# Nine norm totals of a two-layer encoder kernel: from an fp32 product with ones to two fp32r products of a split sum, one slab later

## The reference, cut to what matters

```python
def layer_norm(x, g, b):
    mu = jnp.mean(xf, axis=-1, keepdims=True)
    var = jnp.mean(jnp.square(xf - mu), axis=-1, keepdims=True)
    y = (xf - mu) * lax.rsqrt(var + LN_EPS)
...
    h = causal_dwconv(h, conv_w, conv_b)
    h = jax.nn.silu(layer_norm(h, conv_ln_g, conv_ln_b))
...
        x = layer_norm(DN_ALPHA * x + (1.0 + gate) * y, ln1_g[l], ln1_b[l])
```

## Time and profile before

| | |
|---|---|
| median of 3 runs | 2107.39 us (2107.19 to 2108.32) |
| the profiled execution: its own time | 2107.35 us |
| its span, first to last instruction | 2105.4 us |
| PE busy | 2070.4 us (98%) |
| POOL busy | 1406.3 us (67%) |
| DVE busy | 1189.1 us (56%) |
| ACT busy | 1025.9 us (49%) |
| mean granted TensorE clock | 0.996 |

### The profile page before, as it was taken

The page is one execution under the profiler, slowest core; times in us unless marked ns, Lnnn a source line. Parts: engine busy times, 40 slices in busy tenths (PEclk is TensorE's granted clock), DMA queues, the critical chain, the costliest instruction groups (busy, mean ns, idle before and its releaser), DMA issues.

```text
span 2105.4 us, 27351 instructions
## 1 busy us (share of the span) xinstructions
PE 2070.4 (98%) x9619; PEld 1701.4 (81%) x9619; DVE 1189.1 (56%) x1945; ACT 1025.9 (49%) x1834; POOL 1406.3 (67%) x1773
## 2 busy tenths in 40 slices
PE   7999999999999999999999999999999999999997
PEld 6877778787888888888788888888778888888887
DVE  5888888575515554777632545687651454333235
ACT  3585356555516674374633656234552464433332
POOL 4987767856677887875567885564546776545554
PEclk9999999999999999999999999999999999999999
DMA  8654545533434354553233333332323232434332
GB/s 300 157 134 147 160 128 147 163 110 101 120 110 124 107 162 145 140 159 94 75 105 100 118 103 93 99 106 71 101 73 108 87 104 83 128 100 128 93 93 78
DMA packets 421508, 250.06 MB, mean 119 GB/s; under 512 B 48149, under 2 KB 393085, under 8 KB 421373
## 3 DMA queue, kind: packets, MB, share of 16 engines
q1 hardware_dynamic: 420506, 248.03, 40.1%
q10 hardware_dynamic: 867, 0.29, 0.1%
HBM read 242.71 MB, written 4.26 MB: 117 GB/s over the span
## 4 chain that ended last, share of the span: by engine, by line
PE 80%; POOL 8%; DVE 4%; ACT 4%; issue 3%; DMA 1%; SPq 0%; POOLq 0%; ACTq 0%; DVEq 0%
PE fg L862 25%; PE fg L864 25%; PE fg L863 25%; POOL w_lo L1884 4%; POOL ada_acc L1955 1%; PE bank_s L948 1%; DVE bank_c L1496 1%; ACT ada L1283 1%; DMA stage_in<-in_x_dram 1%; PE bank_l L874 1%; PE bank_t L970 1%; PE bank_l L885 1%; PE bank_t L957 0%; ACT w_hi L1127 0%; POOL ssum L1978 0%
## 5 line engine op out<-in xcount | busy, mean ns | idle before, releaser
L1884 POOL TENSOR_TENSOR w_lo<-raw,w_hi 128x256 fp32r<-128x256 f32 (+1 forms) x1425 | 1032.3, 756 | 626.7 <-ACT w_hi L1127 625.2
L862 PE MATMUL fg<-u_hi,w_hi 128*128 128x512 f32 x2112 | 838.6, 397 | 5.8 <-DVE u_lo L1476 2.1
L864 PE MATMUL fg<-u_hi,w_lo 128*128 128x512 f32 x2112 | 823.7, 390 | 0.0
L863 PE MATMUL fg<-u_lo,w_hi 128*128 128x512 f32 x2112 | 823.4, 390 | 0.0
L1127 ACT ACTIVATE w_hi<-raw 128x1024 fp32r<-128x1024 f32 (+2 forms) x387 | 375.6, 970 | 386.5 <-PE fg L864 282.9
L862 PEld LDWEIGHTS fg<-u_hi,w_hi 128*128 128x128 f32 x2112 | 397.0, 188 | 103.9 <-issue 16.2
L864 PEld LDWEIGHTS fg<-u_hi,w_lo 128*128 128x128 f32 x2112 | 397.0, 188 | 84.6
L863 PEld LDWEIGHTS fg<-u_lo,w_hi 128*128 128x128 f32 x2112 | 397.4, 188 | 81.8 <-issue 2.6
L1496 DVE SCALAR_TENSOR_TENSOR bank_c<-glu,par,bank_c 128x512 f32<-128x512 f32 x448 | 306.1, 747 | 0.1
L1838 DVE SCALAR_TENSOR_TENSOR x<-fg,mod,x 128x512 f32<-128x512 f32 (+1 forms) x168 | 121.6, 724 | 320.0 <-PE fg L864 319.8
L864 PE MATMUL fg<-h_hi,w_lo 128*128 128x512 f32 (+1 forms) x704 | 269.8, 383 | 0.0
(11 more groups left out here) (264 smaller groups left out, 1846.2 us busy)
## 6 DMA issues: line engine op xcount, KB each, us to landing
raw<-in_w_up_dram SPq DMA_DIRECT2D x176, 512.0 KB, 3.8
ada<-in_w_ada_ffn_dram SPq DMA_DIRECT2D x48, 512.0 KB, 4.5
raw<-in_w_down_dram SPq DMA_DIRECT2D x64, 384.0 KB, 3.4
raw<-in_w_in_dram SPq DMA_DIRECT2D x40, 512.0 KB, 3.9
raw<-in_w_down_dram SPq DMA_DIRECT2D x64, 320.0 KB, 3.1
ada<-in_w_ada_mix_dram SPq DMA_DIRECT2D x32, 512.0 KB, 4.3
raw<-in_w_in_dram SPq DMA_DIRECT2D x32, 256.0 KB, 3.8
raw<-in_w_out_dram SPq DMA_DIRECT2D x32, 256.0 KB, 2.9
```

Of the source, the lines that this page charges most:

```text
L862: pe.matmul(out, hi[:, k, :], rhi, start=k == order[0], stop=False)
L863: pe.matmul(out, hi[:, k, :], rlo, start=False, stop=False)
L864: ins = pe.matmul(out, lo[:, k, :], rhi, start=False, stop=k == order[-1])
L1884: ins = pool.tensor_tensor(lo_of(n)[:, ks, :], raw[n % NRAW][:, ks, :], hi_of(n)[:, ks, :].bitcast(F32), ALU.subtract)
```

## The change

For the nine norms, the sum is split before it is totalled. A new step `ch` or `xh` takes the slab that `cm` or `xm` had. In it ACT waits for the finished `ssum` and copies it, rounded, to `sum_hi` (fp32r), and POOL then subtracts `sum_hi` from `ssum` into `sum_lo` (fp32r). `cm` or `xm`, and with it all of `cc` or `xc`, moves one slab on; there PE waits for `sum_lo` and makes two fp32r products with a matrix of ones (`ones_r`), high and low, into the same bank. `cv`, `xv` and what follows keep their slabs. c0 and x0 keep the fp32 product. The entries of c1, x2 and c3 leave `INSIDE`. `sum_lo` takes the memory of `ssum` and `sum_hi` that of `wide`; `ones_r` takes that of three small tiles of the tail and some more.

```diff
 INSIDE = {("cm", 0): 2, ("cv", 0): 4, ("xm", 0): 4, ("xr", 0): 6,
-          ("cm", 1): 2, ("xm", 2): 4, ("cm", 3): 2, ("as", 12): 2, ("as", 18): 2}
+          ("as", 12): 2, ("as", 18): 2}
...
     def conv_norm(mi, ns):
         m, v, r, o = ns
-        put(m, "cm", mi)
+        put(m, "ch", mi)
+        put(m + 1, "cm", mi)
         for k in range(CT):
-            put(m, "cc", mi, k)
+            put(m + 1, "cc", mi, k)
...
     def x_norm(xi, m, c, v, r, per):
-        put(m, "xm", xi)
+        put(m, "xh", xi)
+        put(m + 1, "xm", xi)
         for k in range(DT):
-            put(m + k // c, "xc", xi, k)
+            put(m + 1 + k // c, "xc", xi, k)
...
+            def total_of_parts(n):
+                pe.wait_ge(set_par, 4)
+                pe.wait_ge(total_lo, n)
+                pe.matmul(bank_l[:], ones_r[:], sum_hi[:], start=True, stop=False)
+                return pe.matmul(bank_l[:], ones_r[:], sum_lo[:], start=False, stop=True)
...
             def x_stat(what, xi):
                 if what == "xm":
-                    pe.wait_ge(xsum, (DT - 1) * (xi + 1))
                     take("l", xcenter, DT * (xi + 1))
-                    total().then_inc(xstat, 1)
+                    if xi:
+                        total_of_parts(PARTED["x", xi]).then_inc(xstat, 1)
+                    else:
+                        pe.wait_ge(xsum, DT - 1)
+                        total().then_inc(xstat, 1)
...
+            def sum_high(turn):
+                act.wait_ge(*summed(turn))
+                act.wait_ge(*spread_before(turn))
+                act.activation(sum_hi[:], ssum[:], ACT.Copy).then_inc(total_hi, 1)
...
+            act.activation(ones_r[:], ones_1, ACT.Copy).then_inc(set_par, 1)
...
+                    elif what in ("ch", "xh"):
+                        sum_high((what[0], step[1]))
...
+            def sum_low(turn):
+                pool.wait_ge(total_hi, PARTED[turn])
+                pool.tensor_tensor(sum_lo[:], ssum[:], sum_hi[:].bitcast(F32), ALU.subtract).then_inc(total_lo, 1)
...
+                    elif what in ("ch", "xh"):
+                        sum_low((what[0], step[1]))
```

More of the change, by code:

```diff
@@ L158 @@
          ("x", 5), ("x", 6), ("x", 7)]
+NORM_TURNS = [t for t in TURNS if t[0] != "i"][:-1]
+PARTED = {t: n + 1 for n, t in enumerate(t for t in NORM_TURNS if t[1])}
 NCHUNK = 3 * D // T
@@ L479, in build @@
         tmp = sb("tmp", [P, 2, T])
+        with ExitStack() as region:
+            sum_lo = sb("sum_lo", [P, T], F32R, stack=region)
+            sum_hi = sb("sum_hi", [P, T], F32R, stack=region)
         ssum = sb("ssum", [P, T])
@@ L495, in build @@
         st = sb("st", [P, 2, 7, QT])
-        stats = sb("stats", [P, TB, 2, 6])
-        moments = sb("moments", [P, TB, 2])
-        shift = sb("shift", [P, 2, TB])
+        with ExitStack() as region:
+            stats = sb("stats", [P, TB, 2, 6], stack=region)
+            moments = sb("moments", [P, TB, 2], stack=region)
+            shift = sb("shift", [P, 2, TB], stack=region)
+        ones_r = sb("ones_r", [P, P], F32R)
         with ExitStack() as region:
@@ L584, in build @@
         tr_done, t_copied, pv_done, ahi, alo = (sem(n) for n in ("tr_done", "t_copied", "pv_done", "att_hi", "att_lo"))
+        total_hi, total_lo = sem("total_hi"), sem("total_lo")
         in_const, in_taps, in_sinks, in_pos, tab_out = (sem(n) for n in ("in_const", "in_taps", "in_sinks", "in_pos", "tab_out"))
@@ L631, in freeing, with summed, spread_before @@
             return freed[FREE[P_][0]], FREE[P_][1]
+        def summed(turn):
+            kind, i = turn
+            return (csum, (CT - 1) * (i + 1)) if kind == "c" else (xsum, (DT - 1) * (i + 1))
+        def spread_before(turn):
+            kind, i = NORM_TURNS[NORM_TURNS.index(turn) - 1]
+            return (cstat if kind == "c" else xstat), 3 * (i + 1)
         def copied(c):
@@ L913, in c_stat @@
                 if what == "cm":
-                    pe.wait_ge(csum, (CT - 1) * (mi + 1))
                     take("l", ccenter, CT * (mi + 1))
-                    total().then_inc(cstat, 1)
+                    if mi:
+                        total_of_parts(PARTED["c", mi]).then_inc(cstat, 1)
+                    else:
+                        pe.wait_ge(csum, CT - 1)
+                        total().then_inc(cstat, 1)
                 elif what == "cv":
```

## The result

The changed kernel takes 2123.84 us (median of 4 runs, 2123.15 to 2125.48) beside 2107.29 for the kernel before (4 runs, 2106.84 to 2108.32): a ratio of 1.0081, 95% interval 1.0068 to 1.0094. It is slower, as forecast, but by 16.6 us where 6.2 were forecast, and outside the range of 2109 to 2117.5.

The account below looks back on a forecast made before the run. PE was taken to bound the kernel, busy 2070.4 of 2105.4 us. Savings of 9.3 us against 4.1 of products, 9.0 of waits and 2.5 of restarts gave +6.3 us: 2113.6 us forecast, range 2109 to 2117.5.

Parts of the forecast that it names:

- What goes: PE at the nine norms: dropping the fp32 totals, with their waits for the sum, saves 9.3 us.
- The products and waits: PE at the nine totals: two fp32r products each add 4.1 us in all; eight waits for `sum_lo` add 9.0 us.
- Starting again: PE behind each of eight waits for `sum_lo`: 0.31 us lost before full flow, 2.5 us in all.
- The long stop: An earlier, longer PE wait for an activation part, whose 0.31 us loss was taken as the price of each restart.
- The sum on PE: Savings, new products, waits and restarts at the nine totals together: +6.3 us on PE.
- costed at nothing: ACT's copies, POOL's subtractions, squares a slab later, the copy of `ones_r` and the shifted memory layout: no cost.
- No wait: Rival at the totals: POOL's subtraction ends before PE comes, only savings and new products remain; 2102.2 us, 8%.
- Absorbed: Rival: PE's later stops shrink by what it now waits at the totals, no change; 2109 us, 13%.
- Later waits too: Rival: squares a slab later reach `xv` or `cv` late, at two to four norms by 1 to 2 us; 2116 to 2120 us, 10%.

Follow-up runs that it names:

- b_moved: Kernel before with the nine fp32 totals one slab later and none inside a slab, nothing split: 2106.77 us, ratio 0.9998.
- a_pad64: Changed kernel with 64 bytes of padding behind `ones_r`, so `h` lies 256 bytes from its old place: 2113.04 us, ratio 1.003.
- b_pad192: Kernel before with an empty 192-byte tile ahead of the convolution tiles, shifting `h` as the change did: 2118.75 us, ratio 1.0055.
- a_hi_only: Changed kernel with 64 bytes of padding behind `ones_r`, PE making only the high product, POOL's subtraction unused: 2101.6 us, ratio 0.9976.
- a_late2: Changed kernel with 64 bytes of padding behind `ones_r`, totals done behind the 2nd tile of the slab after the next: 2104.08 us, ratio 0.9986.
- a_late4: Changed kernel with 64 bytes of padding behind `ones_r`, totals done behind the 4th tile of the slab after the next: 2104.17 us, ratio 0.9986.
- b_w_off32: Kernel before with 32 bytes of padding ahead of the weight tiles and 32 behind them: 2151.25 us, ratio 1.021.
- b_all_off64: Kernel before with 64 bytes of padding behind `x`, so `u`, the weights and `h` move together: 2107.97 us, ratio 1.0003.
- b_pad64: Kernel before with an empty 64-byte tile ahead of the convolution tiles: 2111.15 us, ratio 1.0023.
- b_w_off192: Kernel before with 192 bytes of padding ahead of the weight tiles and 64 behind them: 2121.89 us, ratio 1.0071.
- b_w_off64: Kernel before with 64 bytes of padding ahead of the weight tiles and 64 more behind them: 2141.87 us, ratio 1.0168.
- b_pad128: Kernel before with an empty 128-byte tile ahead of the convolution tiles: 2118.88 us, ratio 1.0062.
- b_u_off64: Kernel before with `u` moved by 64 bytes, the weights and `h` by 128: 2138.27 us, ratio 1.0151.

## Why the prediction failed in its size

**What goes: right.** The steps between last products show what the nine totals cost before and what stands in the next slab now (us):

| | c1 | x1 | x2 | c2 | x3 | x4 | c3 | x5 | x6 | sum |
|---|---|---|---|---|---|---|---|---|---|---|
| removed, measured | 0.90 | 1.09 | 1.23 | 0.87 | 1.09 | 0.90 | 1.25 | 1.09 | 0.90 | 9.3 |
| removed, forecast | 0.87 | 1.10 | 1.21 | 0.87 | 1.10 | 0.90 | 1.21 | 1.10 | 0.90 | 9.3 |
| added, measured | 1.25 | 1.98 | 2.01 | 0.45 | 2.05 | 1.89 | 0.96 | 1.99 | 1.84 | 14.4 |
| added, forecast | 1.28 | 2.16 | 2.24 | 0.45 | 2.16 | 2.00 | 1.06 | 2.16 | 2.00 | 15.5 |

**The products and waits: right.** Two products cost 0.45 (c2, which does not wait, shows them alone). The eight waits come to 8.5 us for 9.0; x1 waits 1.29 for 1.40, since the chain from the end of slab 102 to the end of the subtraction is 641.29 - 634.33 = 6.96 us, not 7.07. POOL's subtraction takes 1.26 to 1.29 us; the 1.1 estimated from the Trainium skill's "GPSIMD Engine Reference", section 3.1, does not hold for it.

**Starting again: too large.** Forecast 0.31 a wait, 2.5 in all. Left of 14.4 after waits (8.5) and products (4.1) is 1.8 us, 0.22 each. At x1 the second product starts at 641.75, 0.46 behind POOL's end, where 0.23 would be full flow. The long stop was not the right price. The Trainium skill's rule that PE's queue can pull a weight load ahead ("TensorE: Matmul & The Clock Gate", the array as 16 sub-arrays) is not what made it smaller: the load began at 641.41, only when the wait was over.

**The sum on PE: nearly right.** At the totals +5.1 where +6.3 was forecast. To that come two knock-ons of 0.7 and 0.25 us. Neither was in the sum. The 0.7 is PE's wait for POOL's modulation sum at slab 130; b_moved has it too (0.8 us by the starts), without any subtraction, so it belongs to the later place of the norms. The prediction named these sums, but looked at loads and squares, not at the PE step that reads them. The 0.25 at slab 182 is not in b_moved, but in all kernels that split the sum; no run here tests its cause. The changed kernel without its shift, a_pad64, takes 2113.04 us; the forecast was 2113.6. That they are so near is in part luck: in the trace of a_pad64 the nine places give 5.4 us, 0.9 under the forecast, and the two knock-ons give the 1.0 back.

**The step that failed** is the last of what was costed at nothing: "The memory layout moves by less than a tile; no row prices that, nothing from below and nothing from above is what I take, as no instruction changes its shape". Shape was the wrong thing to look at. A shift of 192 bytes made each product with `h` 6.6 ns slower, 1992 times: 11.1 us of net cost in the trace, 12.1 us by b_pad192 where the shift is the only edit. No row of the trace before could price it, as the distances in all projections of that kernel are multiples of 256; the bound from above should have been left open and the range made wider. The rows could have warned in one way: some two thousand full-width products at one pace are a term in which 3% weigh more than all that the change does at its nine places.

**The rivals.** *No wait* is what a_hi_only builds, by leaving the low product and its wait out: 2101.6 us, near its 2102.2, but with nine products (2.0 us) fewer than that rival has. The kernels with both products and hardly a wait, a_late2 and a_late4, take 2104.1 and 2104.2. *Absorbed* did not happen: the waits elsewhere hardly shrank (`h_lo` from 0.9 to 0.7 us, `probs_t` from 1.9 to 1.8, `w_lo` 0.8 both times). *Later waits too* did not happen at `xv` or `cv`; the delay of a slab that it rests on did cost something, but at slab 130, and only 0.7 us.

**What stays open.** Why the distance counts inside the chip: only its pattern was measured, at six distances and with fp32r operands of these shapes. Whether an fp32 or a bf16 product feels it was not tried, nor whether POOL could subtract ahead of `split_lo`, by which the waits would end without moving the total. The shift costs 10.8 us by the medians of the changed kernel and a_pad64, and 12.1 by those of b_pad192 and the kernel before beside it; the intervals overlap, so I don't tell these apart.

## What to carry to other kernels

When an edit changes the size of any tile in a kernel that PE bounds, compare the addresses of PE's operands before and after as well as the instructions, and measure the change once more with padding that restores them: here the shift cost more than the whole edit. Read PE's pace from starts many products apart, for each operand, since the duration column does not show it. Work given to an engine that does other things first in program order comes only after these, so ask a product that needs it to come half a slab later, and then look who waits further down.

## What the runs showed of the hardware

The pace of fp32r products (128x128 weights, 128x512 streamed, back to back) depends on the distance between the starts of the streamed and the weight tile in a partition, modulo 256 bytes:

| distance | ns per product | seen in |
|---|---|---|
| 0 | 226.7 | before, a_pad64, b_all_off64 |
| 32 | 233.3 | b_w_off32, `h` |
| 64 | 229 | b_pad64, b_w_off192, b_w_off64 `h` |
| 128 | 232.7 | b_pad128 |
| 192 | 233.3 | after, b_pad192, b_u_off64 `u` |
| 224 | 233.3 | b_w_off32, `u` |

At 64 the products are not evenly spaced: in b_pad64 most follow the one before by 226, 229 or 232 ns, 229 in the mean. Half-width products went the other way, from 120 ns at 0 to 113 at 192. The whole effect, `u` and `h` both at a bad distance from the weights, was 43.7 us of 2107.55 (b_w_off32). An fp32 total in full flow costs 0.87 to 0.90 us of PE (before, b_moved), the two fp32r products in its place 0.45 between slabs (after, c2) and 0.53 inside one (a_late4). A PE that had waited 0.3 to 1.3 us for `sum_lo` lost some 0.22 us more in starting again (after).
